# Regrouping the front of a one-core transformer kernel: four mixed groups, column groups, whole modulation chunks, a fifth tile place

## The reference, cut to what matters

```python
c_act = jax.nn.silu(c)
mod = c_act @ w_ada[l] + b_ada[l]                      # 2048 -> 6 * 2048
sh1, sc1, gt1, sh2, sc2, gt2 = jnp.split(mod[:, None, :], 6, axis=-1)
h = rmsnorm(x, g_mix[l]) * (1.0 + sc1) + sh1
x = x + gt1 * hybrid_mixer(h, w_in[l], ...)
h = rmsnorm(x, g_ffn[l]) * (1.0 + sc2) + sh2
x = x + gt2 * conv_glu_ffn(h, w_gate, w_up, conv_w, conv_b, w_down)
```

## Time and profile before

| | us |
|---|---|
| median of 3 runs | 3101.52 |
| lowest, highest | 3099.47, 3101.6 |
| the profiled execution's own time | 3100.88 |
| its span from first to last instruction | 3099.1 |
| busy: PE, DVE, ACT, POOL | 3033.9, 1999.3, 1496.7, 104.8 |

### The profile page before, as it was taken

How to read it: one execution, slowest core, us unless ns; L and a number is a source line. 1 busy time by engine, 2 the same in 40 slices (tenths; PEclk the granted TensorE clock), 3 DMA queues, 4 the chain that set the end, 5 groups by cost and what they waited for, 6 DMA issues and landing times.

```text
span 3099.1 us, 38332 instructions
## 1 busy us (share of the span) xinstructions
PE 3033.9 (98%) x14098; PEld 2523.6 (81%) x14098; DVE 1999.3 (65%) x2277; ACT 1496.7 (48%) x1769; POOL 104.8 (3%) x202
## 2 busy tenths in 40 slices
PE   6899998999999999999999999999999999999999
PEld 5677877888888888888888888888888888888887
DVE  7989888865665666775555565565475655565564
ACT  4555545444544444545444444544545444444543
POOL 2211111100000000000000000000000000000000
PEclk9999999999999999999999999999999999999999
DMA  9988896855556555554556545555455555555555
GB/s 396 387 321 301 315 376 248 341 189 189 184 183 195 187 189 186 166 182 164 193 173 191 177 162 191 169 191 186 167 183 170 192 175 193 171 165 191 170 183 190
DMA packets 179429, 657.11 MB, mean 212 GB/s; under 512 B 19904, under 2 KB 20192, under 8 KB 178528
## 3 DMA queue, kind: packets, MB, share of 16 engines
q1 hardware_dynamic: 151008, 551.28, 52.8%
q0 software_dynamic: 28288, 103.98, 8.9%
HBM read 653.09 MB, written 2.10 MB: 211 GB/s over the span
## 4 chain that ended last, share of the span: by engine, by line
PE 90%; DVE 5%; DMA 2%; issue 1%; ACT 1%; SPq 0%; DVEq 0%; ACTq 0%
PE pg L1039 28%; PE pg L1041 28%; PE pg L1040 28%; DVE R L1606 2%; DMA w_raw<-w 2%; PE pm L1074 1%; DVE w_lo L1679 1%; PE pm L1102 1%; PE pm L1492 1%; DMA R<-w_ada 1%; PE pm L1386 0%; ACT w_hi L579 0%; PE pm L1442 0%; PE pm L1083 0%; PE pm L1116 0%
## 5 line engine op out<-in xcount | busy, mean ns | idle before, releaser
L1541 DVE TENSOR_TENSOR w_lo<-w_raw,w_hi 128x1024 fp32r<-128x1024 f32 x888 | 1085.7, 1225 | 973.7 <-ACT w_hi L500 969.3
L500 ACT ACTIVATE w_hi<-w_raw 128x1024 fp32r<-128x1024 f32 x888 | 940.7, 1060 | 1329.9 <-PE pg L1041 1304.2
L1039 PE MATMUL pg<-w_hi,hT_hi 128*128 128x512 f32 x3200 | 1265.6, 396 | 52.5 <-DVE w_lo L1679 36.5
L1041 PE MATMUL pg<-w_hi,hT_lo 128*128 128x512 f32 x3200 | 1251.4, 391 | 0.0
L1040 PE MATMUL pg<-w_lo,hT_hi 128*128 128x512 f32 x3200 | 1251.0, 391 | 0.0
L1039 PEld LDWEIGHTS pg<-w_hi,hT_hi 128*128 128x128 f32 x3200 | 604.5, 189 | 183.5 <-issue 32.8
L1041 PEld LDWEIGHTS pg<-w_hi,hT_lo 128*128 128x128 f32 x3200 | 604.0, 189 | 127.3
L1040 PEld LDWEIGHTS pg<-w_lo,hT_hi 128*128 128x128 f32 x3200 | 604.8, 189 | 121.7
L1039 PE MATMUL pg<-w_hi,y_parts 128*128 128x512 f32 x864 | 337.6, 391 | 1.4 <-issue 1.4
L1041 PE MATMUL pg<-w_hi,y_parts 128*128 128x512 f32 x864 | 336.3, 389 | 0.0
L1040 PE MATMUL pg<-w_lo,y_parts 128*128 128x512 f32 x864 | 336.1, 389 | 0.0
(11 more groups left out here) (284 smaller groups left out, 1398.5 us busy)
## 6 DMA issues: line engine op xcount, KB each, us to landing
w_raw<-w SPq DMA_DIRECT2D x1028, 512.0 KB, 3.9
R<-w_ada POOLq DMA_DIRECT2D x192, 512.0 KB, 7.4
R<-mem_T SPq DMA_DIRECT2D x4, 512.0 KB, 10.2
x_rows<-x SPq DMA_DIRECT2D x1, 2048.0 KB, 16.2
R<-mem_T SPq DMA_DIRECT2D x1, 2048.0 KB, 12.0
out<-x_rows SPq DMA_DIRECT2D x4, 512.0 KB, 5.0
con_sb<-con SPq DMA_DIRECT2D x1, 1344.0 KB, 16.1
small_w_sb<-small_w POOLq DMA_DIRECT2D x2, 576.0 KB, 5.7
```

Source lines behind the costliest of these rows:

```text
L500: act.activation(w_hi[:, g % RING, :, :].rearrange("p c n -> p (c n)"), raw[:, g % RING, :], ACT.Copy).then_inc(hi_done, 1)
L1039: pe.matmul(out, hi, w_hi[:, slot, c, :], start=start, stop=False)
L1041: return pe.matmul(out, lo, w_hi[:, slot, c, :], start=False, stop=stop)
L1541: tt(flat(w_lo[:, g % RING, :, :]), raw[:, g % RING, :], flat(w_hi[:, g % RING, :, :]).bitcast(F32), ALU.subtract).then_inc(lo_done, 1)
```

## The change

1. **Order and mixed groups.** `mk1` moves ahead of `mv0`; the mixed groups become four, `y`, `p`, `q0`, `x`, over tiles 24 to 55, so stage s is due at tile 24 + 4s.
2. **Columns.** Six of the nine groups (`COLUMNS`) are computed with the weights as stationary operand and the activations as moving one: 24 matmuls of 256 columns a tile in place of 12 of 512. The result has channels on partitions; the transposes of `x`, `y`, `q0`, `q1`, `k0`, `k1` and their second copies go. The convolution on DVE reads the bank of `x` itself, and `v0`, the next group of that bank, waits for it.
3. **Whole chunks.** `weigh` takes 128 x 2048 at once (1 MB, `D` numbers a row); 80 chunks in place of 160 halves in the front, 16 in place of 32 behind it. Places: four, then six of which two lie in the SBUF tile of `x` (from chunk 14, once TensorE has transposed `x`), then four, from chunk 60 two and a half. `x` is loaded again by POOL behind chunk 61, and the residuals wait for it.
4. **When they are weighed.** 32 early chunks at tiles 2 to 45; then 9 over 13 tiles from 47, 9 over 25 from 60, 7 over 10 from 85, 10 over 18 from 95, and 13 over 18 from 113.
5. **Fifth tile place** until tile 100, in SBUF slot 18.
6. **Small banks.** `o2` and `o3` use the banks `pm2,3` and `pm0,1`; they wait no more for the residuals of `o0` and `o1`.
7. **Moves.** The squares and sums of the memory keys go from DVE to ACT (16 activations of 128 x 128 with a running sum). The small weights are issued at tile 44 and the constants at tile 52. The first attention's logits move from tile 69 to 71, the recurrence's last steps on DVE go behind its logits, and the second attention's move from 93 to 91.

```diff
-FRONT = ("mk0", "mv0", "mk1", "x", "y", "p", "q0", "k0", "v0", "q1", "k1", "v1", "o0", "o1", "o2", "o3", "mv1")
+FRONT = ("mk0", "mk1", "mv0", "y", "p", "q0", "x", "k0", "v0", "q1", "k1", "v1", "o0", "o1", "o2", "o3", "mv1")
+COLUMNS = ("y", "q0", "x", "k0", "q1", "k1")
+MIXED = 4
-BANK = {"mk0": 0, "mv0": 1, "mk1": 0, "x": 1, "y": 0, "p": 2, "q0": 1, "k0": 0, "v0": 1, "q1": 0, "k1": 1, "v1": 0,
-        "o0": 1, "o1": 0, "o2": 1, "o3": 0, "mv1": 1}
+BANK = {"mk0": 1, "mk1": 0, "mv0": 1, "y": 0, "p": 2, "q0": 3, "x": 1, "k0": 0, "v0": 1, "q1": 0, "k1": 1, "v1": 0,
+        "o0": 1, "o1": 0, "o2": 2, "o3": 3, "mv1": 1}
-F_TILES += [(F_X + i, j) for j in range(GT) for i in range(3)]
+F_TILES += [(F_MIX + i, j) for j in range(GT) for i in range(MIXED)]
+RAW_PLACE = [g % (RAW_DEEP if g < RAW_DEEP_TO else RING) for g in range(FT)]
...
+def ada_slots(n):
+    if n < X_FROM:
+        first = (14, 16, 4, 6)[n % 4]
+    elif n < X_TO:
+        first = (X_HOME, X_HOME + 2, 4, 6, 14, 16)[(n - X_FROM) % 6]
+    elif n < X_LEFT:
+        first = (X_HOME, X_HOME + 2, 14, 16)[(n - X_TO) % 4]
+    else:
+        return tuple(sorted(14 + (2 * (n - X_LEFT) + h) % 5 for h in range(2)))
+    return (first, first + 1)
...
-        EARLY_FEEDS = [2 + 38 * i // EARLY for i in range(EARLY)]
+        LATE = ((47, 9, 13), (60, 9, 25), (85, 7, 10), (95, 10, 18), (113, 13, 18))
+        WEIGH_FEEDS = [2 + 45 * n // EARLY for n in range(EARLY)]
+        WEIGH_FEEDS += [at + span * i // count for at, count, span in LATE for i in range(count)]
...
+                if n == X_FROM:
+                    pool.wait_ge(rowsT_ps, GT)
+                if n == X_LEFT + 1:
+                    pool.wait_ge(ada_used, X_LEFT)
+                    pool.dma_start(x[:, :, :], t["x"]).then_inc(x_back, 16)
...
+            def column_passes(out, k, slot, c, b):
+                hi, lo = (w[:, slot, c, b * P:(b + 1) * P] for w in (w_hi, w_lo))
+                pe.matmul(out, hi, hT_hi[:, k, :], start=k == 0 and b % 2 == 0, stop=False)
+                pe.matmul(out, hi, hT_lo[:, k, :], start=False, stop=False)
+                return pe.matmul(out, lo, hT_hi[:, k, :], start=False, stop=k == KD - 1 and b % 2 == 1)
...
-                dve.tensor_tensor_reduce(chunk, chunk, c_rows[:, h, :], 1.0, start, ALU.mult, ALU.add,
+            def weigh(n):
+                dve.tensor_tensor_reduce(chunk, chunk, c_rows, 1.0, V("b_ada")[:, n:n + 1], ALU.mult, ALU.add,
                                          mod[:, n:n + 1]).then_inc(ada_used, 1)
...
-            transposes(Zq[0], (0, 1), T_ps)
-            transposes(Zk[0], (2, 3), T_ps)
-            attn_at(69, 0, Zv[0], 8, 0)
+            attn_at(71, 0, Zv[0], "k0", 0)
...
-                head_squares(flat(mk_tok[l]), flat(mk_sq[l]), 0, 8)
+                dve.wait_ge(mem_ss, l + 1)
```

More of the change, by code:

```diff
@@ L66 @@
 FT = len(F_TILES)
+RAW_PLACE = [g % (RAW_DEEP if g < RAW_DEEP_TO else RING) for g in range(FT)]
+RAW_TURN = [RAW_PLACE[:g + 1].count(p) for g, p in enumerate(RAW_PLACE)]
+RAW_BEFORE = [max((m for m in range(g) if RAW_PLACE[m] == p), default=None) for g, p in enumerate(RAW_PLACE)]
 G_FF = len(FRONT)
@@ L76, with ada_loads, ada_turn, ada_before @@
 BLOCKS += [5 * KD + k for k in range(KD)]
[L77 to L81, removed]
+EARLY = M_GATE1
+def ada_slots(n):
[8 more added lines that the diff above has]
+    return (first, first + 1)
+def ada_loads(n):
+    a, b = ada_slots(n)
+    return [(a, 0, D)] if b == a + 1 else [(a, 0, AH), (b, AH, D)]
+def ada_turn(slot, n):
+    return sum(load[0] == slot for m in range(n + 1) for load in ada_loads(m))
+def ada_before(n):
+    return max((m for m in range(n) if set(ada_slots(m)) & set(ada_slots(n))), default=None)
 IN2 = 15
@@ L363, in build @@
         mem_in = [sem(f"mem_in{i}") for i in range(4)]
-        ada_in = [sem(f"ada_in{i}") for i in range(len(ADA_SLOTS))]
+        ada_in = {i: sem(f"ada_in{i}") for i in sorted({load[0] for n in range(len(BLOCKS)) for load in ada_loads(n)})}
         raw_in = [sem(f"raw_in{i}") for i in range(RING)]
+        front_in = [sem(f"front_in{i}") for i in range(RAW_DEEP)]
         out_stored = sem("out_stored")
@@ L1105, in outs, with heads_of @@
                     i.then_inc(o_ps, 1)
+            def heads_of(v):
+                return [v[:, h, :, :] for h in range(NH)]
             def y_T(occ, rows):
@@ L1140, in upto, with attn_at @@
                         k = j * KC + c
-                        for tb in range(TB):
-                            i = passes(front_bank(u, tb), hT, k, tb, done % RING, c, k == 0, k == KD - 1)
+                        if FRONT[u] in COLUMNS:
+                            for b in range(4):
+                                i = column_passes(front_bank(u)[:, b // 2, b % 2 * S:(b % 2 + 1) * S], k, done % RING, c, b)
+                        else:
+                            for tb in range(TB):
+                                i = passes(front_bank(u, tb), hT, k, tb, done % RING, c, k == 0, k == KD - 1)
                     i.then_inc(tile_used, 1)
                     done += 1
-            def attn_at(t, occ, v, t_value, forget):
+            def attn_at(t, occ, v, keys, forget):
                 upto(t)
-                pe.wait_ge(T_sb, t_value)
+                pe.wait_ge(evac_act, F_ACTS[FRONT.index(keys)])
                 for h in range(NH):
@@ L1178, in _ @@
             pe.wait_ge(hn_ready, 1)
[L1179 to L1180 removed]
+            transposes(mk_tok[0], (0, 1), T_ps)
+            upto(23)
             pe.wait_ge(T_sb, 2)
@@ L1761, in _ @@
             mem_normed(0)
-            for s in range(4):
-                upto(20 + s)
-                gain_stage(s)
-            for s in range(3):
-                upto(24 + s)
-                mixed_low(s)
+            upto(20)
+            mem_squares(1)
+            gain_stage(0)
+            upto(21)
+            gain_stage(1)
+            upto(22)
+            gain_stage(2)
+            upto(23)
+            mem_normed(1)
+            upto(24)
+            mixed_low(0)
+            gain_stage(3)
@@ L2370 @@
     out1 = column_tiles(a["w_out"][0][order])
-    stream = [memory[0], memory[1][:GT]]
+    stream = [memory[0][:GT], memory[1][:GT], memory[0][GT:]]
     columns = [column_tiles(w1[:, c:c + NW]) for c in starts]
-    stream += [columns[u - F_X][j][None] for u, j in F_TILES if F_X <= u < F_OUT]
+    stream += [columns[u - F_MIX][j][None] for u, j in F_TILES if F_MIX <= u < F_OUT]
     stream += [out1[(u - F_OUT) * GT + j][None] for u, j in F_TILES if F_OUT <= u < F_OUT + NB]
```

493 lines of the change are left out of this document (255 added, 238 removed).

## The result

The changed kernel takes **3112.49 us** (median of 6 runs, 3108.13 to 3119.23), the kernel before 3100.33 us beside it (6 runs, 3098.66 to 3101.6): a ratio of 1.004, 95% interval 1.003 to 1.0051. It is slower by 12 us, where 3092 was forecast and 3104 was the upper end. The profiled execution took 3108.13 us with a span of 3106.3, 7.2 more than the span before; the median lies 4.4 above it, since the changed kernel's runs spread over 11 us where those of before spread over 3.

A forecast was written before the change was run, and what follows sets the result against it. DMA and DVE together were taken to bound the first 56 tiles, TensorE those to 95, DVE the front's end. Terms -10.6 - 5.3 + 4 + 1 - 3.5 + 5 = -9.4 us from 3101.5 gave 3092 us, range 3072 to 3104.

The forecast's parts named there:

- Late chunks: Tiles 113 to 132: 13 chunks (29.5 us) on DVE's list in place of 19 halves (24.4 us); loss 5 us, 2 to 8.
- Rival D: Late stretch: each last chunk waits 1 us for DMA, DVE's chain ends 13 us later, 3105 us; chance 0.06.
- Reload of `x`: 2 MB on POOL's queue near tile 99, needed at tile 113; costs nothing, up to 6 us.
- Bytes to tile 56: Start to tile 56: evenly requested chunks remove DMA pauses, tile 56 near 203 us; gain 10.6 us, from 3 to 22.
- Column matmuls: 24 matmuls of 256 columns a tile at 0.121 us each; hidden in `y`, `q0`, `x`, otherwise loss 4 us, from 0.
- rival C: Column matmuls show their weight loads, 33 us above the forecast if half hidden, kernel slower at 3125 us; chance 0.07.
- Transposes: On TensorE: six groups of 8 transposes go; gain 5.3 us.
- attention: First attention: TensorE's 3.5 us of waits for exponentials go; gain 3.5 us, 0 to 5.
- squares: ACT's squares ahead of tiles 12 and 20, some 4 us in one piece; loss 1 us, 0 to 4.
- Small banks: TensorE freed at tile 112 but then waits for late data and DVE; zero, or a 5 us gain if DVE's chain were short.
- A: DMA delivers 410 to 420 GB/s, DVE bounds, tile 56 at 192 to 195 us, kernel 3079 us; chance 0.25.
- B: No change, 3100 us: DMA bounds to tile 56 (gain only 3 us), and late bytes cost 3; chance 0.2.

The follow-up runs named there:

- experiment 5: Changed kernel with three whole places for the late chunks (60 to 79) in place of two and a half: 3107.83 us, ratio 1.0023 to the kernel before.
- experiment 2: Changed kernel with 9 chunks in place of 13 over the last 18 tiles, more of them from tile 60: 3094.66 us, ratio 0.9982 to the kernel before.
- experiment 6: Changed kernel with 6 chunks in place of 13 over the last 18 tiles, more of them from tile 60: 3090.32 us, ratio 0.997 to the kernel before.
- Experiment 9: Kernel before, with `x` loaded again (2 MB) on POOL's queue and the residuals waiting for it: 3100.01 us, ratio 0.9997.
- Experiment 7: Changed kernel with the 1.3 MB of late constants issued behind tile 128 in place of tile 112: 3109.18 us, ratio 1.0029 to the kernel before.
- experiment 1: Changed kernel with every chunk loaded as two halves but still weighed whole: 3119.63 us, ratio 1.0064 to the kernel before.
- experiment 3: Changed kernel with four tile places throughout in place of five until tile 100: 3122.5 us, ratio 1.0069 to the kernel before.
- experiment 4: Changed kernel with the old banks for `o2` and `o3`: 3112.6 us, ratio 1.0044 to the kernel before.
- experiment 8: Kernel before, with 26 of its half chunks in place of 19 in the last 18 tiles: 3109.04 us, ratio 1.003.
- experiment 12: Changed kernel with experiment 5's places, experiment 6's lists, fifth tile place until tile 130, first 14 chunks as halves, late constants behind tile 128: 3076.91 us.

## Why the prediction was wrong, step by step

*Late chunks: the step that failed.* The prediction put +5 us on 13 chunks at the end, for DVE's work, and had their data in time, so that it gave the waits for them nothing. Counted from tile 113 on, DVE took 13.5 us more: its busy time grew by 6.8 us, inside the bounds of 2 to 8, and the waits for chunks cost 6.7 (experiment 5 takes them away). "DVE full from tile 113 to 132, in 69 us" came true for the busy time alone; the stretch took it 78. One sign of being wrong was named and came: DVE idle for chunks after tile 95. That these chunks are the cause is shown by experiments 2 and 6, in which fewer of them at the end make the changed kernel faster than the kernel before.

What had been left out is the places. Before, five halves could be under way; from chunk 60 on it is two and a half chunks. These are the same bytes, but DVE must be done with the chunk two or three before a chunk until POOL may ask for it, and the one that DVE waited for took 8.3 us to land (the chain above). The prediction had also seen how little room there was: 48.5 MB to bring from tile 95 on, 121 us at 400 GB/s, in stretches that had taken 123.5 us (60.1 + 63.4 in the earlier trace rows; it writes 124.5).

*Rival D.* Its mechanism and its place were right, and its chance of 0.06 was too low. Its price was not right: it named 13 us of waits where 6.7 came, and it said that such waits decide from 10 us on. The kernel got slower with fewer of them, since it also lost 4.4 us of its lead and 2.0 behind tile 132, which no rival had.

*The whole difference.* The forecast was -9.4 us, the profiled executions give +7.2, which is 16.6 more. Up to tile 95 the lead was 12.7 us where the terms of the sum give 14.4: 1.7. In the late part 17.9 us (4.4 + 6.8 + 6.7) stand for 5: 12.9. Behind tile 132 it is 2.0.

*Reload of `x`.* It was costed at nothing, up to 6 us. Experiment 9 bears this out beside five places; what it costs beside two and a half was not tried by itself.

*The lead and tile 113.* The prediction took it that the lead at tile 95 goes on to the end. 4.4 us of it went: 2.5 before SP issued the block of 3.3 MB, for a reason that stays open, and 1.9 behind it, where POOL's queue took more of the DMA engines than before. Experiment 7, with 1.3 MB less in that block, has 5.2 us less of the wait for tile 113, so the wait is for these bytes; the kernel before waits for them too.

*Bytes to tile 56: right mechanism, too large.* 10.6 us forecast; tile 56 starts at 212.4, and 5.5 us of forget-gate matmuls lie ahead of it now, so that 206.9 compares with 213.6: 6.7 us. To tile 24 the forecast was 97 to 104 and nothing was gained (109.5), in part since chunks of 8 KB rows crowd out the first tiles; halves there give 105.7 (experiment 1), still short of the forecast. From tile 24 to 56 DMA's share is 1.01 at 406 GB/s, as forecast, but this is owed to the fifth place (386 GB/s without it, experiment 3), which the prediction named only as cover.

*Column matmuls: the pace right, the cover wrong.* Rows of the changed kernel's timeline of TensorE:
```profile
129.82 0.28 PE L1201 MATMUL pm<-hT_hi,w_hi 128*128 128x256 f32 x1
129.94 0.28 PE L1202 MATMUL pm<-hT_lo,w_hi 128*128 128x256 f32 x1
130.06 0.28 PE L1203 MATMUL pm<-hT_hi,w_lo 128*128 128x256 f32 x1
...
131.02 0.28 PE L1202 MATMUL pg<-hT_lo,w_hi 128*128 128x256 f32 x1
```
Ten of them take 1.20 us: 0.120 us each, 0.121 was forecast; rival C is out. The Trainium skill, TensorE: Matmul & The Clock Gate, Part 3: Packing small matmuls — row/col tiling, says that a weight load overlaps a running matmul only where the row groups differ; by that sentence each load would be bare here, and the trace contradicts it. The same section also has loads into a background weight buffer pulled ahead of running matmuls, which would fit; no run here shows which it is. But "the 24 tiles of `y`, `q0`, `x` lie where DMA is the bound, and hide it" is doubtful: 24 x 2.88 us and 8 x 2.73 are 91 of the 102.9 us there, with 5.5 of gate matmuls 96.5, and TensorE is busy for 98.7. DMA and TensorE had become equals there, so the 3.6 us by which column tiles are dearer (24 x 0.15) may have counted. This is argued; no run has these groups computed the old way.

*Transposes, attention, squares, chunks.* From tile 56 to 95 the time fell from 153.2 us (142.4 with the 10.8 ahead of tile 56) to 147.2 (141.7 with the 5.5): 6.0 us, where the forecast has 5.3 + 3.5 - 4 = 4.8. TensorE's 3.5 us of waits for exponentials are gone, and it waits for nothing in that stretch (busy 141.80 of 141.80 above). The 16 squares on ACT take 7.7 us with their reads of sums, 3.9 a piece, where some 4 were set, and nobody waited for them:
```profile
L618 ACT ACTIVATE R<-R 128x128 f32<-128x128 f32 x16 | 4.7, 296 | 0.1
L618 ACT ACTIVATION_READ_ACCUMULATOR R<-R 128x1 f32 x16 | 3.0, 187 | 0.0
```
A whole chunk takes 422.19 - 419.92 = 2.27 us from start to start, as forecast:
```profile
419.92 2.35 DVE L1684 CUSTOM_DVE_ANT_0 R<-R,vec_sb 128x2048 f32<-128x2048 f32 x1
422.19 0.08 DVE L1684 DVE_READ_ACCUMULATOR2_ANT mod<- 128x1 f32 x1
```

*Small banks.* Zero at the end, as forecast (experiment 4).

*Rivals A and B.* A had the DMA engines deliver more: 406 GB/s between tiles 24 and 56, but tile 56 far from the 192 to 195 us that it names. B put 3 us on late bytes where 6.7 us of waits came, and had the first part gain 3 us; it gained 6.7, which lies halfway between B and the forecast.

**What stays open.** The 2.0 us behind tile 132, of which TensorE's waits for `w_lo` there make 1.2 (3.7 in place of 2.5); that part takes 2608.3 us in experiments 8 and 12 and 2616.0 in experiment 1, which nothing here explains. The 2.5 us of lead lost between tile 95 and the block. Why the changed kernel's runs spread more. And of the 3.9 us for each late chunk between 13 and 9, how much is the chunk's own late landing and how much the tile's.

## What to carry to other kernels

Count a resource's list where the chain ends, not over the whole: DVE had 24 us of idle time between tiles 56 and 95, and behind tile 113 the kernel before had left it 2. Seven chunks of 2.27 us on the wrong side of that line (and two more between tiles 95 and 112) are the difference between a gain of 10 us and a loss of 12. When pieces get larger, count how many can be under way: two and a half places of 1 MB are as many bytes as five of 512 KB, but a freed place comes back half as often. A lead is not carried to the end by itself: of 12.7 us at tile 95, 8.3 were left at tile 113, and part of that loss came from a second queue which had meanwhile been given larger rows.

## What the runs showed of the hardware that was not expected

- **Two full queues get through equally many rows, so the larger row takes the larger share.** From 18 to 23 us it was 188 packets to 188 with rows of 8 KB on POOL's queue and 4 KB on SP's, and 282 to 284 with 4 KB on both. SP's 512 KB pieces came 3.76 and 2.56 us apart (experiment 1). The Trainium skill, DMA: Bandwidth & Descriptors, Measured (HBM→SBUF, 128 partitions, SWDGE, issued from GpSimd), asks for pieces of 1 MiB or more; in the first 14 chunks the smaller ones gave the earlier tiles, and the rate of all queues together was no lower (387 GB/s in the changed kernel to tile 24, 394 in the kernel before, with halves).
- **A fifth place for tiles is worth 10 us**, nearly all of it in 32 tiles (experiment 3), with no byte fewer to move.
- **The pace of 256-column matmuls was a little slower with more columns of weights**: 0.1136, 0.1175 and 0.120 us for 8, 72 and 128, all at a granted clock of 1.00. These are three different places of the program, so that the columns are the reason is not shown.
